# Stick-breaking layer: items walked two by two, one older value product ahead of the two scores

## What is computed

```
def stick_breaking_block(q_blk, k_ctx, v_ctx, q0):
    z = jnp.einsum('bthd,bshd->bhts', q_blk, k_ctx) * (SB_HEAD_DIM ** -0.5)
    before = jnp.arange(s_len)[None, :] < (q0 + jnp.arange(tq))[:, None]
    log_keep = jnp.where(before, jax.nn.log_sigmoid(-z), 0.0)
    csum = jnp.cumsum(log_keep, axis=-1)
    weights = jnp.where(before, jnp.exp(jax.nn.log_sigmoid(z) + csum[..., -1:] - csum), 0.0)
    return jnp.einsum('bhts,bshd->bthd', weights, v_ctx)
```

## Time and profile before

| | |
|---|---|
| median of 3 runs | 3864.09 us (3859.55 to 3866.41) |
| span of the profiled execution | 3862.8 us |
| TensorE matmuls busy | 3735.6 us, 97% |
| VectorE, ScalarE, GpSimd busy | 61%, 43%, 44% |
| stick-breaking items, groups 0 to 7 | about 3115 to 3771 us of the span |

### The profile page before, as it was taken

How to read it: one execution, slowest core, us unless ns; L and a number is a source line. 1 busy time by engine, 2 the same in 40 slices (tenths; PEclk the granted TensorE clock), 3 DMA queues, 4 the chain that set the end, 5 groups by cost and what they waited for, 6 DMA issues and landing times.

```text
span 3862.8 us, 50418 instructions
## 1 busy us (share of the span) xinstructions
PE 3735.6 (97%) x19892; PEld 3040.4 (79%) x19892; DVE 2372.8 (61%) x3104; ACT 1653.3 (43%) x2799; POOL 1689.3 (44%) x1108
## 2 busy tenths in 40 slices
PE   8999999999999899999999899999999999999998
PEld 6888887666655466888887799999878988888877
DVE  7667685633555548667684767554577156666664
ACT  5333444322222335333444553411572356666663
POOL 4555554344444535555553243422532233443464
PEclk9999999999999999999999999999999999999999
DMA  3234574200000121234574011221121300000024
GB/s 121 96 109 150 194 247 135 88 23 28 22 17 17 50 85 57 96 113 153 202 238 133 29 44 44 65 89 61 48 69 56 134 32 23 30 25 28 28 69 140
DMA packets 143917, 327.30 MB, mean 85 GB/s; under 512 B 16896, under 2 KB 20512, under 8 KB 143296
## 3 DMA queue, kind: packets, MB, share of 16 engines
q1 hardware_dynamic: 132368, 281.80, 21.9%
q0 software_dynamic: 8752, 39.65, 2.7%
q10 hardware_dynamic: 2560, 2.61, 0.2%
HBM read 252.37 MB, written 71.63 MB: 84 GB/s over the span
## 4 chain that ended last, share of the span: by engine, by line
PE 78%; DVE 13%; ACT 5%; POOL 2%; issue 2%; DMA 0%; ACTq 0%; DVEq 0%; SPq 0%; POOLq 0%
PE ps L958 6%; PE ps L959 6%; PE ps L960 6%; PE ps L414 5%; PE ps L415 5%; PE ps L416 5%; PE ps L4316 4%; PE ps L978 3%; PE ps L977 3%; PE ps L976 3%; PE ps L4248 2%; PE ps L4250 2%; PE ps L4249 2%; PE ps L2059 2%; PE ps L4300 2%; PE ps L2061 2%
## 5 line engine op out<-in xcount | busy, mean ns | idle before, releaser
L388 POOL TENSOR_TENSOR wlo<-raw,whi 128x1024 fp32r<-128x1024 f32 x154 | 377.1, 2453 | 483.9 <-ACT whi L379 483.7
L414 PE MATMUL ps<-xh,whi 128*128 128x352 f32 (+1 forms) x1400 | 473.3, 338 | 7.4 <-DVE xl L671 2.7
L415 PE MATMUL ps<-xh,wlo 128*128 128x352 f32 (+1 forms) x1400 | 450.6, 322 | 0.0
L416 PE MATMUL ps<-xl,whi 128*128 128x352 f32 (+1 forms) x1400 | 450.1, 321 | 0.0
L861 POOL TENSOR_TENSOR fwl<-fpb,fwh 128x512 fp32r<-128x512 f32 x204 | 302.3, 1491 | 267.1 <-ACT fwh L851 266.8
L861 POOL TENSOR_TENSOR fwl<-fpa,fwh 128x512 fp32r<-128x512 f32 x202 | 293.6, 1462 | 278.9 <-ACT fwh L851 278.8
L4621 POOL TENSOR_TENSOR ospl<-osp,osph 128x672 fp32r<-128x672 f32 (+4 forms) x144 | 190.9, 1326 | 357.9 <-ACT osph L4442 356.8
L414 PEld LDWEIGHTS ps<-xh,whi 128*128 128x128 f32 x1400 | 265.4, 190 | 19.2 <-POOL wlo L388 6.6
L415 PEld LDWEIGHTS ps<-xh,wlo 128*128 128x128 f32 x1400 | 264.3, 189 | 8.0 <-issue 2.2
L416 PEld LDWEIGHTS ps<-xl,whi 128*128 128x128 f32 x1400 | 264.1, 189 | 0.0
L958 PE MATMUL ps<-fxh,fwh 128*128 128x512 f32 x640 | 249.3, 390 | 1.3 <-ACT u L1036 1.3
(11 more groups left out here) (505 smaller groups left out, 9708.4 us busy)
## 6 DMA issues: line engine op xcount, KB each, us to landing
raw<-in_w_dram SPq DMA_DIRECT2D x154, 512.0 KB, 3.7
hs_scratch<-u SPq DMA_DIRECT2D x176, 256.0 KB, 2.4
u<-hs_scratch SPq DMA_DIRECT2D x118, 256.0 KB, 2.9
fpa<-in_fg_dram SPq DMA_DIRECT2D x88, 256.0 KB, 3.8
fpb<-in_fg_dram SPq DMA_DIRECT2D x88, 256.0 KB, 3.8
fpa<-in_fd_dram SPq DMA_DIRECT2D x88, 256.0 KB, 3.5
fpb<-in_fd_dram SPq DMA_DIRECT2D x88, 256.0 KB, 3.7
acc<-hs_scratch SPq DMA_DIRECT2D x80, 256.0 KB, 2.7
```

Source lines behind the costliest of these rows:

```text
L388: pool.x.tensor_tensor(K.wlo[n % 3][:, :], K.raw[n % 2][:, :], K.whi[n % 3][:, :], ALU.subtract).then_inc(*S.up("w_lo", n))
L414: pe.x.matmul(out, wh, xh, start=k == 0, stop=False)
L415: pe.x.matmul(out, wl, xh, start=False, stop=False)
L416: last = pe.x.matmul(out, wh, xl, start=False, stop=k == K - 1)
```

## The change

`step` now takes two items at once. The order in a step of items n and n+1 is: mix of n-4; z of n, z of n+1; a turn; mix of n-3; then twice (for the first and the second item m of the pair): copy of it, sums of the item two before it, four fill steps, rest of that item, soft of it; then the weight's low part and gate loads. On TensorE that reads: mix(n-4), z(n), z(n+1), mix(n-3), sums(n-2), fill, rest(n-2), sums(n-1), fill, rest(n-1). Buffers, banks and all instructions stay as they are. The "hi unit" entries keep their places after items 1, 7 and 13. In the last group "begin 8" comes after item 7 instead of item 5, and the casts are put in pairs.

```diff
@@ -4131,28 +4131,25 @@
 
 def _odd_places():
 
-    out, pipe = [], [None] * 5
-
-    def step(it, lo_unit):
-        pipe.insert(0, it)
-        if pipe[1]:
-            out.append(("soft", pipe[1]))
+    out, pipe = [], [(), (), ()]
+
+    def step(items, lo_unit):
+        pipe.insert(0, items)
+        out.extend(("mix", it) for it in pipe[2][:1])
+        out.extend(("z", it) for it in items)
+        for it in items:
+            if it[1] < 7 and it[0] % PER_T in (12, 14, 16):
+                out.append(("turn", (it[1] + 1, it[0] % PER_T // 2 - 6)))
+        out.extend(("mix", it) for it in pipe[2][1:])
+        for m in range(2):
+            out.extend(("copy", it) for it in items[m:m + 1])
+            out.extend(("sums", it) for it in pipe[1][m:m + 1])
+            out.append(("fill", 4))
+            out.extend(("rest", it) for it in pipe[1][m:m + 1] if it[3])
+            out.extend(("soft", it) for it in items[m:m + 1])
         if lo_unit is not None:
             out.append(("lo unit", lo_unit))
-        if it is not None:
-            out.append(("z", it))
-            if it[1] < 7 and it[0] % PER_T in (12, 14, 16):
-                out.append(("turn", (it[1] + 1, it[0] % PER_T // 2 - 6)))
-            out.append(("copy", it))
-        if pipe[3]:
-            out.append(("mix", pipe[3]))
-        if pipe[2]:
-            out.append(("sums", pipe[2]))
-        out.append(("fill", 4))
-        if pipe[2] and pipe[2][3]:
-            out.append(("rest", pipe[2]))
-        if pipe[4] and not pipe[4][3]:
-            out.append(("gate", 3 * pipe[4][1] + pipe[4][2] + 2))
+        out.extend(("gate", 3 * it[1] + it[2] + 2) for it in pipe[2] if not it[3])
         pipe.pop()
 
     unit = UNIT_AT["Q.8"] + 3
@@ -4160,35 +4157,34 @@
         if t < 7:
             out.append(("begin", t + 1))
         lo_unit = None
-        for m, it in enumerate(ODD[PER_T * t:PER_T * (t + 1)], 1):
-            step(it, lo_unit)
+        for m in range(0, PER_T, 2):
+            step(ODD[PER_T * t + m:PER_T * t + m + 2], lo_unit)
             lo_unit = None
-            if t < 7 and m % 6 == 2:
+            if t < 7 and m % 6 == 0:
                 unit += 1
                 lo_unit = unit
                 out.append(("hi unit", unit))
             if t == 7:
-                out.extend(LAST_PAIR.get(m, ()))
+                out.extend(LAST_PAIR[m // 2])
         if t < 7:
             out.append(("fill", 1000))
-    for _ in range(4):
-        step(None, None)
+    for _ in range(2):
+        step((), None)
     out.extend([("fill", 1000), ("part", (2, 4)), ("rows", (2, 0)), ("rows", (2, 1))])
     return out
 
 
-LAST_PAIR = {m: [("part", (0, m - 1))] for m in (1, 2, 3, 4)}
-LAST_PAIR[5] = [("part", (1, 0))]
-LAST_PAIR[6] = [("part", (0, 4)), ("begin", 8)]
-LAST_PAIR[4].append(("rows", (0, 0)))
-LAST_PAIR[7] = [("rows", (0, 1)), ("part", (1, 1))]
-LAST_PAIR[8] = [("part", (1, 2))]
-LAST_PAIR[9] = [("rows", (1, 0)), ("part", (1, 3))]
-LAST_PAIR[10] = [("part", (2, 0))]
-LAST_PAIR[11] = [("part", (2, 1))]
-LAST_PAIR[12] = [("part", (1, 4))]
-LAST_PAIR[13] = [("rows", (1, 1)), ("part", (2, 2))]
-LAST_PAIR[14] = [("part", (2, 3))]
+LAST_PAIR = {
+    0: [("part", (0, 0)), ("part", (0, 1))],
+    1: [("part", (0, 2)), ("part", (0, 3)), ("rows", (0, 0))],
+    2: [("part", (1, 0))],
+    3: [("part", (0, 4)), ("begin", 8), ("rows", (0, 1)), ("part", (1, 1))],
+    4: [("part", (1, 2))],
+    5: [("rows", (1, 0)), ("part", (1, 3)), ("part", (2, 0))],
+    6: [("part", (1, 4)), ("part", (2, 1))],
+    7: [("rows", (1, 1)), ("part", (2, 2))],
+    8: [("part", (2, 3))],
+}
 ODD_PLACES = _odd_places()
```

## The result

The changed kernel is slower: 3894.52 us, the median of four runs (3893.61 to 3896.71), against 3864.6 us for the kernel before beside it (3859.55 to 3866.41). The ratio is 1.0078, 95% interval 1.0063 to 1.0092. The forecast was 3863.4 and its range ended at 3877.

The account below looks back on a forecast made before the run. TensorE's own stream and new waits on it were taken as the bound. Terms -15.5 + 4.6 + 1.4 + 0.7 + 5.1 + 3.0 = -0.7 us gave a span of 3862.1, a median of 3863.4; range 3851 to 3877.

Parts of the forecast that it names:

- What bounds the kernel: TensorE, busy 81.2 of 81.6 us a group: only its own stream and new waits on it count.
- Changes of array shape: On TensorE, switches between full array, row halves and column halves: 91 fewer at 0.17 us each, 15.5 us less.
- The direct change from value product to score: TensorE going from column halves to row halves, 71 times: taken as one change; free or double shifts 12 us either way.
- The second score behind the max: TensorE's second score of a pair waits for VectorE's max to free its bank: 0.65 us a group, 4.6 in all.
- S: The moment after the last fill matmul's slot, from which the forecast reckons when cast, low part and max run.
- rival B: VectorE's queue becomes the pair's clock: max 0.4 us later, five of six evicting pairs wait, about 3879; chance 0.11.
- Turning the values: TensorE's fill waits for VectorE's copy of the transposed values, behind two mins: 0.2 us more a group, 1.4 in all.
- The carry: TensorE's "rest" waits for VectorE's add: 0.1 us late in pair (6,7), 0.7 us over seven groups.
- Both cost nothing while POOL has its idle half: Later weight low parts and moved gate loads cost nothing; otherwise 0 to 3 us, kept in the range.
- The last group: Eight items without fill instead of six: waits of 9.3 us instead of 4.2, 5.1 more, worst 1.7 in (6,7).
- The clock: TensorE's granted clock drops in the last group: 3 us taken, between 0 and 10; under 0.78 over a longer stretch.

Follow-up runs that it names:

- e1: The changed kernel with a third softplus buffer (osp n%3) instead of two; 3856.06 us, 0.9973 of the kernel before, a group of 79.88 us.
- e9: The changed kernel, two softplus buffers, with the max of a pair's second item ahead of the second fill; 3863.02 us, 1.0000 of the kernel before.
- e8: The changed kernel with third softplus buffer, transposes between a pair's two scores, and last group item by item; 3840.59 us, 0.9936 of the kernel before.
- e6: The changed kernel with third softplus buffer and both older value products behind the two scores, none ahead; 3878.59 us, 1.0032 of the kernel before.
- e3: The changed kernel with pairs only in groups 0 to 6, the last group item by item as before; 3883.94 us, 1.0047 of the kernel before.
- e4: The kernel before with pairs only in the last group, groups 0 to 6 item by item; 3874.45 us, 1.0023 of the kernel before.
- e2: The changed kernel, two softplus buffers, with the value transposes between the two scores of a pair; 3879.84 us, 1.0036 of the kernel before.
- e7: The changed kernel with third softplus buffer and the last group item by item with the old places; 3845.38 us, 0.9954 of the kernel before.

## Why the prediction was wrong

- **What bounds the kernel: right.** TensorE's own stream and new waits on it, nothing else, as the windows after show.
- **Changes of array shape: right.** 0.17 forecast, 0.19 measured by the labels (e1). The direct change from value product to score is one change: the product of 144 columns at 3343.61 leads to scores at 3344.01, 0.40 later as the forecast had it with one change's 0.11, and with the usual 0.26 between their first two pairs. The 12 us either way that the range held for it were not needed. The Trainium skill (TensorEngine Tiling (Array Packing), Key Properties) says that a change of tiling mode drains TensorE; these rows agree in that this kind costs a gap like the others.
- **The second score behind the max: right in kind.** 0.45 forecast after (12,13), 0.34 found, in that place only: 2.4 us in seven groups for the 4.6 of the sum. The max ends at 3345.01, S+1.98, against S+1.99 reckoned from the earlier trace rows. So rival B's condition (the max later than S+2.0) did not come, though its time of 3879 was nearest: it named VectorE's queue, but by another link. Its price doesn't follow from its own words either: five pairs x 0.4 x 7 is 14 us, not 17. The eviction in front of the max, which it rests on, is a link of the chain that did hold (e9), with a max that was on time. VectorE's throughput is no bound: e1 does the same work in 79.88 us a group.
- **Turning the values: this step failed.** "The copy then stands behind two mins instead of one" counted their 0.81 each and took the mins to start when their scores are there. The second one starts 1.8 us later, held by POOL's low part: a wait that the forecast put at nothing without a reason. Forecast 0.2 more a group, measured 1.32 + 1.15 = 2.5 more, beside the 0.34 of the earlier trace rows at item 12, which is unchanged. Seven groups: 17.3 us instead of 1.4.
- **The carry: failed by the same omission.** "It is 0.1 late in (6,7)": 1.01 measured, and e1 has none. Seven groups: 7.1 us instead of 0.7.
- **"Both cost nothing while POOL has its idle half"** priced POOL by its busy share. Its low part was a link in VectorE's chain at an idle moment of POOL. It also looked only at POOL's moved entries, not at who waits for POOL. The wait stood in the code of the kernel before, and its trace had it three times, 4.5 us, in the list of VectorE's waits; the rows that the forecast rests on list the waits of TensorE alone.
- **Waits cost more than their label.** By the labels a group has 4.16 - 0.34 = 3.82 us of waits more and 2.06 of changes less: 81.6 + 1.8 = 83.4. It took 84.3. e1 has the same order, so no price of a change enters there: it is 4.45 shorter with three waits of 3.48 less, and 0.97 is in no label. The rows say where it is. The label counts from the modelled end of the matmul before, which lies 0.16 past the start of the next one where nothing waits (0.32 long, 0.16 apart); and after a held fill the second matmul follows by 0.26 (3349.13 to 3349.39), not 0.16. By that estimate a wait costs 0.26 more than its label. With every wait taken off at that price four orders agree on what a change of shape costs, also an estimate: 81.00 us for 67 changes (before), 78.68 for 56 (e1), 78.87 for 57 (e8, no waits), 76.73 for 47 (e6, seven waits of 4.67 in all), 0.21 each.
- **The last group: near in sum, in part by luck.** The waits on the add are 9.8 for 9.3, but not in the forecast's places. The seven without fill make 8.0, the two worst, 1.8 each, in pairs (0,1) and (2,3) and not in (6,7); the other two, 1.3 and 0.6, are in pairs (14,15) and (16,17), where the forecast had the add 0.6 us early. The held min is in these too: with the third buffer (e1, 3660 to 3800) seven waits of 6.4 are left (the line below). From the first score of the group to the end it is 181.8 us before, 188.6 after (6.8 more, where 5.1 + 3.0 less 2.4 for 14 changes of array shape, 5.7, was forecast), but 184.5 in e1: 4.2 of the 6.8 go with the buffer. Without the held min the forecast would have been 3 us too dear here.

```profile
PE ps L4367 <- DVE oz L4599: 6.4, 7, 1.1
```

- **The clock: as expected in kind.** It was under 0.78 over a longer stretch: 0.68 over 41.2 us (3703.8 to 3745). Before, it was 0.78 over 24 us and 0.50 over the 6 behind them, 0.72 over these 30. As the lower level is 0.50, these means say that some 26 us were spent at it after and 17 before, an estimate. What that cost (3.0 in the forecast) no run measures by itself.

```profile
3681.00:3705.00 24.00, 19.85 (x117) 13.31 (x118) 14.76 (x28) 15.91 (x30) 14.68 (x13) 0.78 0.12 39
3705.00:3711.00 6.00, 6.00 (x30) 5.46 (x28) 3.53 (x5) 4.57 (x7) 4.02 (x4) 0.50 0.00 0
```

A group by these terms: -2.3 for the changes of shape, +3.8 for the labels of the waits, +1.0 for what four more waits cost beyond them, 2.5 of the 2.7 found; seven groups are 19.1 us slower. The forecast had -13.1 + 4.6 + 1.4 + 0.7 = -6.4 for them. The range was too narrow for one reason: it was built from the terms that were listed, and the largest was not on the list.

Open: how much of the last group's cost is the clock and how much the waits (no run holds one fixed), and what the seam in e3 and e4 costs. The 12 us by which the start of the layer scatters between profiles has no explanation here. The medians hold it, so the readings rest on the groups and on the spans from the first score.

## What to carry to other kernels

Before items are issued in pairs, list from the code every wait that each moved operation makes, on every engine, also those that the trace shows as never holding: a two-deep buffer whose release chain (here eviction, max, cast, low part) fits into one item's distance holds the queue when the next two uses come together. On an in-order engine a held operation is paid by whatever stands behind it, so ask of each new wait on the main engine what its releaser was itself waiting for, and fix that; moving the victim (e2) only moves the wait. An order that loses can be right in its aim: with one more buffer of 2816 bytes per partition it turned from +0.8% to -0.3%, and with two small moves more to -0.6%. A term that comes out near its forecast is no proof of it: the last group's did, with a wait in it that the forecast did not know.

## What the runs showed of the hardware that was not expected

- A wait costs TensorE more than the idle time before the instruction, 0.26 us by the rows at 3349.13 and 0.3 each by e1 against after. From e7 to e8 1.0 us went where two labels made 0.68 and a change of shape came in.
- Changing how the array is divided costs TensorE about 0.2 us in these groups, at the full clock and mostly 320 to 352 columns, also when it goes straight from column halves to row halves.
- Three waits of 1.0 to 1.3 us in the 84 us of a group left the granted clock at 1.00. In the last group, with TensorE busy 33.2 of 41.2 us and seven waits of 0.4 to 1.8 us in them, it was 0.68 on average between its two levels, 1.2 and 2.4 GHz.
